# First items operand tile by operand tile over four banks, and second-mixer keys split without GpSimd

## The reference

```python
def first_block(x, ...):
    h = concatenate([meta, x])
    for l in range(2):
        hn = rmsnorm(h, g[0])
        mix = hgrn2_mixer(hn, ...) if l == 0 else fox_mixer(hn, w_q, w_out, k_sh, v_sh, c_sh)
        h = h + rmsnorm(mix, g[1])
        h = h + rmsnorm(conv_ffn(rmsnorm(h, g[2]), ...), g[3])

def fox_mixer(x, w_q, w_out, k, v, c):          # 16 heads of 64
    q = (x @ w_q)
    logits = einsum("bhqd,bhkd->bhqk", q, k) / sqrt(64) + (c_q - c_k)
    p = softmax(where(mask, logits, -1e30))
    return einsum("bhqk,bhkd->bhqd", p, v) @ w_out

def second_block(x, c, ...):
    for layer in range(2):
        mod = silu(c) @ ada_w[layer] + ada_b[layer]     # shift, scale, gate of mixer and of ffn
        h = rmsnorm_2(x, g) * (1.0 + scale_m) + shift_m
        y = gdn_mixer(h, ...) if layer == 0 else mla_mixer(h, ...)
        x = x + gate_m * y
        h = rmsnorm_2(x, g) * (1.0 + scale_f) + shift_f
        x = x + gate_f * ((silu(h @ w_gate) * (h @ w_up)) @ w_down)
    return rmsnorm_2(x, g_final)
```

## Time and profile before

| what | us |
|---|---|
| median of 3 runs | 1596.88 (1595.53 to 1597.49) |
| profiled execution | 1595.38 |
| its span | 1593.6 |
| PE busy | 1469.6 |
| VectorE busy | 1041.1 |
| ScalarE busy | 779.9 |
| GpSimd busy | 281.6 |

### The profile page before, as it was taken

The page is one execution under the profiler, slowest core; times in us unless marked ns, Lnnn a source line. Parts: engine busy times, 40 slices in busy tenths (PEclk is TensorE's granted clock), DMA queues, the critical chain, the costliest instruction groups (busy, mean ns, idle before and its releaser), DMA issues. The chain is left out here.

```text
span 1593.6 us, 29023 instructions
## 1 busy us (share of the span) xinstructions
PE 1469.6 (92%) x11301; PEld 1404.5 (88%) x11301; DVE 1041.1 (65%) x1727; ACT 779.9 (49%) x1272; POOL 281.6 (18%) x384
## 2 busy tenths in 40 slices
PE   5999879999788898999998899989999989999997
PEld 4999769999686667999997789989999987899997
DVE  5664678877765447788757755357787665677643
ACT  5655644454454444555545555564443555534341
POOL 0000101220053330121100153102332100132110
PEclk8999999999998899999998999999999998999999
DMA  6432535659431224465771311236765733275451
GB/s 275 176 126 106 192 122 193 233 188 335 177 139 74 80 104 162 166 234 211 255 252 58 132 54 54 68 121 222 277 248 208 242 106 137 99 291 185 145 181 44
DMA packets 41141, 265.80 MB, mean 167 GB/s; under 512 B 4561, under 2 KB 5713, under 8 KB 15441
## 3 DMA queue, kind: packets, MB, share of 16 engines
q1 hardware_dynamic: 41040, 264.44, 46.0%
HBM read 263.38 MB, written 1.05 MB: 166 GB/s over the span
## 5 line engine op out<-in xcount | busy, mean ns | idle before, releaser
L224 DVE TENSOR_TENSOR w_lo<-raw,w_hi 128x2048 fp32r<-128x2048 f32 (+2 forms) x207 | 425.4, 2059 | 238.4 <-ACT w_hi L220 234.7
L220 ACT ACTIVATE w_hi<-raw 128x2048 fp32r<-128x2048 f32 (+3 forms) x224 | 385.8, 1727 | 38.1 <-PE bank L398 34.0
L396 PE MATMUL bank<-z_hi,w_hi 128*128 128x258 f32 x752 | 215.4, 286 | 5.1 <-DVEq L931 4.2
L397 PE MATMUL bank<-z_lo,w_hi 128*128 128x258 f32 x752 | 213.0, 283 | 0.0
L398 PE MATMUL bank<-z_hi,w_lo 128*128 128x258 f32 x752 | 212.3, 282 | 0.0
L396 PE MATMUL bank<-x_hi_up,w_hi 128*128 128x272 f32 (+1 forms) x704 | 203.5, 289 | 8.2 <-DVE x_lo_up L688 8.1
L398 PE MATMUL bank<-x_hi_up,w_lo 128*128 128x272 f32 (+1 forms) x704 | 201.7, 287 | 0.0
L397 PE MATMUL bank<-x_lo_up,w_hi 128*128 128x272 f32 (+1 forms) x704 | 201.4, 286 | 0.0
L396 PEld LDWEIGHTS bank<-z_hi,w_hi 128*128 128x128 f32 x752 | 142.1, 189 | 6.7 <-DVE w_lo L224 3.0
L397 PEld LDWEIGHTS bank<-z_lo,w_hi 128*128 128x128 f32 x752 | 143.2, 190 | 0.1
L398 PEld LDWEIGHTS bank<-z_hi,w_lo 128*128 128x128 f32 x752 | 142.4, 189 | 0.0
(11 more groups left out here) (450 smaller groups left out, 3832.1 us busy)
## 6 DMA issues: line engine op xcount, KB each, us to landing
raw<-w_up SPq DMA_DIRECT2D x44, 1024.0 KB, 4.8
raw<-w_gu SPq DMA_DIRECT2D x44, 1024.0 KB, 4.8
work<-w_ada SPq DMA_DIRECT2D x27, 1024.0 KB, 4.9
raw<-w_down SPq DMA_DIRECT2D x32, 704.0 KB, 4.3
raw<-w_dn SPq DMA_DIRECT2D x32, 704.0 KB, 4.1
raw<-w_a_in SPq DMA_DIRECT2D x16, 1024.0 KB, 5.5
mod_w_down<-w_ada SPq DMA_DIRECT2D x12, 1024.0 KB, 6.2
raw<-w_gdn_qkv SPq DMA_DIRECT2D x12, 1024.0 KB, 4.8
```

The costliest lines, as they stand in the source:

```text
L220: act.activation(w_hi[:, s, 0:blocks * P], raw[:, s, 0:blocks * P], ACT.Copy).then_inc(hi_split.sem, 1)
L224: dve.tensor_tensor(w_lo[:, s, 0:blocks * P], raw[:, s, 0:blocks * P], w_hi[:, s, 0:blocks * P].bitcast(F32), ALU.subtract).then_inc(lo_sp ...
L396: pe.matmul(o, w_hi[:, s, b], x_hi[:, xk, cols[0]:cols[1]], start=begin, stop=False)
L397: pe.matmul(o, w_hi[:, s, b], x_lo[:, xk, cols[0]:cols[1]], start=False, stop=False)
```

## The change

Five edits. (1) `hosting`: the modulation column comes at the second item of each group (where groups have 2 or 4 items), not the first. (2) A product whose operand comes tile by tile and that is not one of the down products (a_out, up0, b_out, up1, gdn_out with two items; gu0, gu1, mla_in, those with `root`, with one; mla_out with none) runs its first items together: for each operand tile, all output tiles of these items, over two or four banks. The item is done at its last operand tile; `root.pe_root` comes after the whole first item. (3) The same by hand in the mixers: Hgrn's first item over two banks, Fox's first four query tiles over banks 0, 1, 4, 5, Gdn's gdn_ab and first two key tiles over three. (4) In Fox, ScalarE and VectorE write the halves of 64 rows themselves to fox_heads, fox_keys_hi and fox_keys_lo; GpSimd's casts, fox_high and fox_low are gone, and a head waits for VectorE. (5) ScalarE's final increment of item_out in Fox and Gdn comes a little earlier.

```diff
                 def hosting(r, s):
                     if limited:
-                        return isinstance(r, int) and r - first < hosts * every and (r - first) % every == 0
-                    return (s - first) % SLOTS % every == 0
+                        return isinstance(r, int) and r - first < hosts * every and (r - first) % every == min(1, every - 1)
+                    return (s - first) % SLOTS % every == min(1, every - 1)
...
+                joint = 0 if halves or not (entry or x_ready) else 1 if root else 2
+
                 def tensor(pe):
+                    def joint_items():
+                        for r in range(first + 1, first + joint):
+                            pe.wait_ge(lo_split.sem, r + 1)
+                            pe.wait_ge(item_out.sem, r - 1)
+                        for k in range(k_tiles):
+                            if entry:
+                                pe.wait_ge(entry.split.sem, entry.split.at(k + 1))
+                            if x_ready:
+                                pe.wait_ge(x_ready.sem, x_ready.at(x_step * (k // x_pair + 1) + x_off))
+                            for r in range(first, first + joint):
+                                s = r % SLOTS
+                                for t in range(tiles):
+                                    o = where(r, s, t)[:, 0:width]
+                                    b = slice((t * k_tiles + k) * P, (t * k_tiles + k + 1) * P)
+                                    pe.matmul(o, w_hi[:, s, b], x_hi[:, k, cols[0]:cols[1]], start=k == 0, stop=False)
+                                    pe.matmul(o, w_hi[:, s, b], x_lo[:, k, cols[0]:cols[1]], start=False, stop=False)
+                                    last = pe.matmul(o, w_lo[:, s, b], x_hi[:, k, cols[0]:cols[1]], start=False,
+                                                     stop=k == k_tiles - 1)
+                                if k == k_tiles - 1:
+                                    last.then_inc(item_done.sem, 1)
...
                 def bank_of(event):
-                    return bank[turn[event] % 2]
+                    m = turn[event]
+                    return bank[(0, 1, 4, 5)[m]] if m < 4 else bank[m % 2]
...
+                def halves_of(event):
+
+                    n = index_of(event)
+                    if part_of(event) == "q":
+                        return [(slice(0, dv), heads[0:dv, n, 0, :], heads[dv:P, n, 0, :]),
+                                (slice(dv, P), heads[dv:P, n, 1, :], heads[0:dv, n, 1, :])]
+                    hi, lo = keys_hi[:, n % 3, :, :], keys_lo[:, n % 3, :, :]
+                    return [(slice(dv * a, dv * a + dv), hi[side, a, :], lo[side, a, :])
+                            for a in range(2) for side in (slice(0, dv), slice(dv, P))]
...
                     def head(i):
                         if i < n_heads:
                             t, a = i // 2, i % 2
-                            pe.wait_ge(stacked.sem, stacked.at(4 * KD + 8 * t + 8))
+                            pe.wait_ge(made_low.sem, made_low.at(split_at[tile("k", t)] + 1))
...
-                            act.activation(high[:, u % 2, :], bank_of(event)[:, 0:T1], ACT.Copy,
-                                           scale=0.125 if part_of(event) == "q" else 1.0).then_inc(made_high.sem, 1)
+                            if part_of(event) == "k" and index_of(event) >= 3:
+                                act.wait_ge(scored.sem, scored.at(2 * (index_of(event) - 2)))
+                            for rows, hi, _ in halves_of(event):
+                                last = act.activation(hi, bank_of(event)[rows, 0:T1], ACT.Copy,
+                                                      scale=0.125 if part_of(event) == "q" else 1.0)
+                            last.then_inc(made_high.sem, 1)
...
+                    def first_items():
+                        for r in (first, first + 1):
+                            pe.wait_ge(lo_split.sem, r + 1)
+                        for k_ in range(KD):
+                            pe.wait_ge(entry.split.sem, entry.split.at(k_ + 1))
+                            for i, (r, t, done) in enumerate(((first, 0, item_done), (first + 1, 0, half_done),
+                                                              (first + 1, 1, item_done))):
```

133 lines of the change are left out of this document (75 added, 58 removed).

## The result

The changed kernel takes 1607.9 us in the median against 1596.2 of the kernel before, measured beside it: ratio 1.0095, 95% interval 1.006 to 1.013. It is slower: the medians stand 11.7 us apart, the ratio of 0.95% would be 15 us, its interval 10 to 21. 1593.4 was forecast, with a range up to 1600.5. The four runs lie between 1604.5 and 1618.5 us, those of the kernel before between 1589.2 and 1597.5. The profiled executions stand 9.0 us apart: 1602.6 against 1593.6 us of span.

A forecast was written before the change was run, and what follows sets the result against it. The prediction took the matrix engine PE, busy 92% of a 1593.6 us span, as the bound, leaving its waits and low clock to win. Its terms summed to -3.55 us, giving 1593.4 on the median of 1596.88, range 1588 to 1600.5.

The forecast's parts named there:

- The column in gu1: In gu1, the modulation column one item later removes a 2.87 us wait and the low clock after it: -4.9 us.
- The wait at item 2: In up0 and up1, PE stands 1.7 us for the joined first items' banks: +0.7 and +0.6 us.
- The casts: Second mixer's later heads: removing GpSimd's casts wins nothing beside the probabilities' chain, which grows longer: +2.1 us.
- the third mixer: Third mixer's start: the gates' tile ends later and the first convolution moves 1.9 to 3.4 us: +1.9 us.
- The price of a half: Second mixer: a half-height piece costs as a full-height one, 0.28 us on ScalarE and 0.35 on VectorE.
- The first head: Second mixer up to its first head: keys without casts -3.8 us, queries +0.35, together -3.45.
- the queries: Second mixer's query tiles: two halves instead of one each on VectorE add +0.35 us.
- dn0: After gu0: its last column comes later, at most 1 us on VectorE, hidden by two items of PE: 0.
- b_out: The projection b_out, joined over four banks, has a shorter output, estimated at a third of up0's price: +0.3 us.
- Rival one: Late first items make PE stand and the clock fall at four entries, Gdn at its upper end: 1600.9 us, chance 0.16.
- Rival three: The stall only moves: the column holds gu1's third output, and gu0 as well: +3.1, 1596.5 us, chance 0.20.
- rival two: The second mixer keeps its gain: the 2.1 give-back falls away and 1.86 us waits go: 1589.4 us, chance 0.22.

The follow-up runs named there:

- e13: The changed kernel without its edit of the third mixer's first tiles: 1599.1 us, ratio 1.0048 to the kernel before.
- e5: The kernel before with only the third mixer's first three tiles (gates, two key tiles) run operand tile by operand tile: 1604.8 us, ratio 1.0064.
- e2: The kernel before with the modulation column one item later in gu1 alone: 1590.7 us, ratio 0.9973.
- e4: The kernel before with only the second mixer's queries and keys written as halves by ScalarE and VectorE, without GpSimd's casts: 1602.0 us, ratio 1.0043.
- e7: The kernel before with only the second mixer's first key tile written as halves by ScalarE and VectorE: 1595.2 us, ratio 0.9994.
- e1: The kernel before with only the modulation column one item later, wherever it is hosted: 1592.3 us, ratio 0.9985.
- e10: The kernel before with the column one item later and the products' first items together, mixers unchanged: 1596.9 us, ratio 1.0016.
- e3: The kernel before with only the products' first items run together operand tile by operand tile, column where it was: 1605.7 us, ratio 1.0069.
- e6: The kernel before with the first item alone operand by operand over its own two banks in a_out, up0, b_out, up1, gdn_out: 1595.3 us, ratio 1.0000.
- e11: The kernel before with the edits of e2, e6 and e7 together: 1588.0 us, ratio 0.9953.
- e8: The kernel before with ScalarE reading each second-mixer key tile four times and each query tile twice, at full height: 1601.8 us, ratio 1.0042.
- e12: The kernel before with ScalarE's additional second-mixer reads (three per key tile, one per query tile) at half height, rows 0 to 63: 1603.4 us, one run.

## Why the prediction was wrong, point by point

**What held.** The column in gu1: -4.9 forecast, -4.6 measured alone and -5.2 in the change. The wait at item 2: 1.7 forecast, 1.73 at up0 and 1.70 at up1, and with it up0 +1.0 against +0.7, up1 +1.1 against +0.6. The casts lie beside the chain that holds the probabilities, so their end isn't won: the three waits of 1.86 did vanish, and waits for probabilities did take their place. Each of these was a mechanism read from one row of the trace, and the sizes of the column in gu1 and of the two entries came out within 0.5 us. gu0 gained 2.4 us where 1.8 stood in the sum beside a loss of 0.6.

**The step that failed most: the third mixer, +1.9 forecast, 5.1 found in its two stages (8.8 and 9.4 in the medians of e13 and e5).** The lateness was sized right: the first convolution is 2.2 us later relative to the entry, forecast 1.9 to 3.4. I then took that lateness for the whole price. It isn't: PE does the first 108 matmuls faster than before, has then nothing to do, and stands 4.19 us for the first key sum. Before there was no wait (0.69 in e2). Behind this stand the clock fell, as rows 8 had shown behind one of 2.87 us, and that is another 1.4 us in the changed kernel and 2.9 in e5. I had costed this very thing as a gain in gu1 and not asked whether a new stand elsewhere would cost it. Working out PE's time and the other engines' time separately and taking the later one would have shown the stand.

**The price of a half.** "I price it as the full-height one, 0.28 and 0.35 us": it was 0.40 and 0.45. So a key tile is 1.2 us longer on ScalarE, not 0.85. With both waits of a pair longer (0.75 to 1.27 and 2.0 to 3.65) this is 2.2 us per pair in e4, 6.6 in all, against the 2.1 of the sum. The 0.28 rested on no row for pieces, and the bound I gave to it went only down.

**The first head, -3.45 forecast, -0.3 found.** The -3.8 of the keys held: in e4, with all keys as halves, PE waits 4.33 us for them where it had waited 2.71 and 5.49, 3.9 less, and with the first key tile alone as halves the stage is 4.2 us shorter (e7). The step that failed was the queries, +0.35. With all as halves (e4) the stage is only 1.2 shorter: PE's two waits for query tiles are 1.10 and 3.45 us instead of 0.51 and 2.50, and the low clock behind the second lasts 5.8 us instead of 3.4, together 2.8. With the first four tiles joined the second wait is 4.86. Again outputs fall due together, which I had reasoned out for up0 and not for this place.

**dn0, 0 forecast, +2.7 found.** The prediction has here "at most 1 us on VectorE there, hidden by two items of PE, 0". The column now stands ahead of the last item's product. GpSimd's last low part comes later by it, SP's load of dn0's column waits for that low part, and so VectorE waits 6.18 instead of 2.50 us for the DMA, with a low part and a residual step queued behind. The prediction counted the moved instruction and not what stands behind it: the product, and the load that hangs on it. In e1, with the column alone moved, dn0 loses 1.2; it loses 2.6 with the joint items too (e10).

**b_out and gdn_out.** b_out lost 1.4 against +0.3. I had scaled it by the number of reads instead of following its chain: it has no wait at its third item, but PE's wait for ScalarE ahead of the norm's sums is 5.3 us instead of 4.3 (5.4 in e3 and e10). gdn_out has waits of 0.41 and 0.19 us for its outputs; more isn't shown, since its stage is 167.8 in e10 with the same joint items, within what it varies by. Down0 with the norm after it, +1.0, was no term of mine: 0.4 to 0.5 of it comes with the column, since e1 and e10 have it too (down0 without the norm 76.6 before, 77.0 and 77.1 there). The norm took 9.9 to 10.7 us with unchanged code and 10.8 here.

**The rivals.** Rival one was nearest: 1600.9, from late first items and a falling clock, with Gdn at its upper end. Its place was wrong. At the entries the stand of 1.7 us was never followed by a low clock (e10: 0.29 us matmuls after it); it was in the third mixer, behind 4.2 us. Its price of 1.5 us per entry is therefore not shown. Its premise was thin: of the mixer's stands of 1.86 us only those at 519.87 and 549.85 had a low clock within 5 us of them, that at 581.09 kept it at full speed up to the mixer's end. e6 puts an operand tile's matmuls over two banks, and up0 is 0.95 us shorter, with the low clock as long as before (14 matmuls against 13). The advice for products with few rows in the Trainium skill, TensorE: Matmul & The Clock Gate, "HAM oscillation", to do all K tiles of one output tile before waiting for a DMA so that PE stays at its high clock, is thus not confirmed for this entry. Rival three did not happen: no wait for the third output in gu1. Of rival two, the stages of e7 and e11 show that a gain up to the first head exists (-4.2 us), in another form than the change has it.

**The range** stopped at 1600.5 because each bound was taken alone. Three terms (the entries, the queries and the third mixer) had their downside in one mechanism: outputs that fall due together. They were off in the same direction, and I added them as if they were independent.

## What to carry to other kernels

Running several output tiles together makes their ends coincide. The gain is at most the time for which the engine would have starved, and what it costs is the first output's cover: join no more tiles than the outputs behind them can drain while the next item runs (two banks gave 1 us, four lost 1 to 2.5). When a step is moved, follow what now stands behind it, up to the loads that wait for that. And when an engine gets ahead of its chain, ask where it will stand next, and whether the stand brings the clock down: that may cost more than the time it had won. A profile is one execution: read a stage of 50 us or more with short matmuls from several profiles with the same code before a difference of 2 us is believed.

## What the runs showed of the hardware

ScalarE's copies of 272 columns from a bank to a buffer follow each other every 0.28 us, at 128 rows and at 64 (e8, e12). Four halves whose row halves change, two of them going from rows 0 to 63 to rows 64 to 127 or back, took 0.40 each, VectorE's 0.45. Here the four pieces by row half therefore cost more than four times the step from one copy to the next.

TensorE's granted clock stayed up after stands of 1.7 us at the entries of up0 and up1, and fell to the lower of its two levels after stands of 2.87 (gu1 before), 4.86 (the second mixer's queries) and 4.18 us (the third mixer). The length of a stand doesn't settle it: in gu1 of e4 the clock stayed at full speed after 3.18 us (1417 to 1424). At the start of the fourth mixer's query product the same code stands 2.33 us in every kernel; before, the clock was 0.50 from 1302 to 1304, in the changed kernel 1.00 in the same place (1319 to 1325); and after the next stand, 1.30 and 1.23 us, it was 0.76 (1313 to 1320) against 1.00 (1331 to 1338). Its fourth mixer was 3.9 us shorter by this. In the second mixer's heads, where PE's work between is short, the same code had 111.9 us at a mean granted clock of 0.92 (before) and 116.1 at 0.89 (e10), with the same waits.

With GpSimd's 96 casts gone, the low part beside the first keys took 2.29 us on VectorE instead of 2.42; two others in the mixer had taken 2.41 and 2.47 beside casts, all the rest 2.29 before as well. GpSimd lost more: its first four casts, beside that low part (from 479.85 before), took 3.77 us, the next four 1.83. The Trainium skill, GPSIMD Engine Reference, section 1, says that GpSimd shares its SBUF interfaces with VectorE, and the trace agrees. For VectorE this was 0.12 to 0.18 us at a time, so little was to be won there; the 1.9 us on GpSimd lay within PE's wait of 5.49 us.
